# Four units of seven products in each gate and up block, the lows of one pair made by an adding DMA

## The reference, cut to what matters

```
def swiglu(h, w_gate, w_up, w_down):
    return (jax.nn.silu(h @ w_gate) * (h @ w_up)) @ w_down
x = x + mixed
h = rmsnorm(x, ffn_norm[i])
x = x + swiglu(h, ffn_w_gate[i], ffn_w_up[i], ffn_w_down[i])
```

## Time and profile before

| | |
|---|---|
| median of 3 runs | 2096.81 us |
| the profiled execution | 2097.19 us |
| its span, first to last instruction | 2095.3 us |
| granted TensorE clock | 1.0 of full speed |
| busy: PE, DVE, ACT, POOL | 100%, 81%, 66%, 3% |
| DMA, mean busy share of 16 engines | 66.8% (main queue) |

### The profile page before, as it was taken

The page is one execution under the profiler, slowest core; times in us unless marked ns, Lnnn a source line. Parts: engine busy times, 40 slices in busy tenths (PEclk is TensorE's granted clock), DMA queues, the critical chain, the costliest instruction groups (busy, mean ns, idle before and its releaser), DMA issues.

```text
span 2095.3 us, 28360 instructions
## 1 busy us (share of the span) xinstructions
PE 2090.1 (100%) x9733; PEld 1728.8 (83%) x9733; DVE 1687.6 (81%) x2225; ACT 1392.7 (66%) x1890; POOL 65.7 (3%) x39
## 2 busy tenths in 40 slices
PE   9999999999999999999999999999999999999999
PEld 8888888888888888888888888888888888888887
DVE  5776668798988998889767677776889898988888
ACT  6677647576776677656657677665677677777654
POOL 1111000000000000000011101000000000000000
PEclk9999999999999999999999999999999999999999
DMA  8687557676676667665667768675767666666664
GB/s 283 216 231 197 181 168 214 202 221 209 211 226 219 207 208 210 204 214 178 198 211 228 236 219 250 214 231 187 215 217 229 206 214 216 220 214 203 202 200 141
DMA packets 334454, 442.68 MB, mean 211 GB/s; under 512 B 133936, under 2 KB 136720, under 8 KB 334352
## 3 DMA queue, kind: packets, MB, share of 16 engines
q1 hardware_dynamic: 333936, 441.31, 66.8%
q0 software_dynamic: 320, 0.02, 0.0%
q10 hardware_dynamic: 96, 0.03, 0.0%
HBM read 408.27 MB, written 2.10 MB: 196 GB/s over the span
## 4 chain that ended last, share of the span: by engine, by line
PE 99%; DVE 1%; ACT 0%; issue 0%; ACTq 0%
PE work L1942 17%; PE work L1940 17%; PE work L1941 17%; PE acc L1940 15%; PE acc L1942 14%; PE acc L1941 14%; PE work L2105 1%; PE work L2143 1%; PE work L2055 0%; PE work L2116 0%; PE work L2150 0%; PE acc L1929 0%; DVE w_lo L1511 0%; PE work L2119 0%; ACT p_buf L1395 0%; DVE s_buf L1773 0%
## 5 line engine op out<-in xcount | busy, mean ns | idle before, releaser
L1511 DVE TENSOR_TENSOR w_lo<-raw,w_hi 128x1024 fp32r<-128x1024 f32 x756 | 867.4, 1165 | 103.1 <-ACT w_hi L1228 100.0
L1228 ACT ACTIVATE w_hi<-raw 128x1024 fp32r<-128x1024 f32 x756 | 753.8, 1012 | 275.7 <-PE work L1942 155.5
L1940 PE MATMUL work<-w_hi,xT_hi 128*128 128x512 f32 x1516 | 589.9, 389 | 0.0
L1942 PE MATMUL work<-w_hi,xT_lo 128*128 128x512 f32 x1516 | 589.8, 389 | 0.0
L1941 PE MATMUL work<-w_lo,xT_hi 128*128 128x512 f32 x1516 | 589.7, 389 | 0.0
L1940 PE MATMUL acc<-w_hi,xT_hi 128*128 128x512 f32 (+1 forms) x878 | 341.9, 389 | 0.5 <-DVE w_lo L1511 0.5
L1942 PE MATMUL acc<-w_hi,xT_lo 128*128 128x512 f32 (+1 forms) x878 | 338.5, 386 | 0.0
L1941 PE MATMUL acc<-w_lo,xT_hi 128*128 128x512 f32 (+1 forms) x878 | 338.4, 385 | 0.0
L1942 PEld LDWEIGHTS work<-w_hi,xT_lo 128*128 128x128 f32 x1516 | 284.5, 188 | 59.1
L1941 PEld LDWEIGHTS work<-w_lo,xT_hi 128*128 128x128 f32 x1516 | 284.5, 188 | 59.0
L1940 PEld LDWEIGHTS work<-w_hi,xT_hi 128*128 128x128 f32 x1516 | 284.5, 188 | 59.0
(11 more groups left out here) (183 smaller groups left out, 1944.7 us busy)
## 6 DMA issues: line engine op xcount, KB each, us to landing
raw<-in_ffn_w_down_dram SPq DMA_DIRECT2D x176, 512.0 KB, 4.9
raw<-in_ffn_w_gate_dram SPq DMA_DIRECT2D x160, 512.0 KB, 3.8
raw<-in_ffn_w_up_dram SPq DMA_DIRECT2D x160, 512.0 KB, 4.7
raw<-in_odd_w_in_dram SPq DMA_DIRECT2D x48, 1024.0 KB, 5.6
raw<-in_even_w_in_dram SPq DMA_DIRECT2D x32, 1024.0 KB, 5.8
raw<-in_even_w_out_dram SPq DMA_DIRECT2D x16, 1024.0 KB, 5.0
raw<-in_odd_w_out_dram SPq DMA_DIRECT2D x16, 1024.0 KB, 7.0
bias<-in_bias_dram SPq DMA_DIRECT2D x24, 384.0 KB, 3.7
```

The lines of the kernel that those rows point to most:

```text
L1228: act.activation(w_hi[:, s, 0:out], src, ACT.Copy).then_inc(hi_ready, 1)
L1511: dve.tensor_tensor(w_lo[:, s, 0:out], src, w_hi[:, s, 0:out].bitcast(F32), ALU.subtract).then_inc(lo_ready, 1)
L1940: pe.matmul(out_ps, x_hi, wh, start=start, stop=False)
L1942: return pe.matmul(out_ps, x_lo, wh, start=False, stop=stop)
```

## The change: what it does

- `BLOCK` takes the place of `BODY`: pairs 0, 2, 4 and 6 are "eight", pairs 1, 3, 5 and 7 are "seven". A block starts in the ring's order at pair 5 (`FIRST_K`), as before. It has 24 "spots" (halves), numbered 0 to 23 from pair 0 on.
- Pair 0 leaves the rings `w_hi` and `w_lo`. In `negate` ACT copies its raw weights to `added_hi` and again, with scale -1, to `added_lo`, and POOL issues a DMA that adds the raw weights to `added_lo` (128x1024, `accum_op=ALU.add`). DVE does nothing for this pair. The negates stand at spots 18 and 19, six ahead of their use. SP waits for these DMAs, not for `w_lo`, before it loads over pair 0's slot.
- The splits are placed anew (`splits_of_block`), and so are the sums (`sums_of_block`) and the steps of the join (`JOINS`: mix 0 and 1 at spot 0, 2 and 5 at spot 1, 3 at spot 2, 4 and 6 at spot 3, 7 at spot 7). `hidden` stands at spots 6 and 7, `hidden_words` at 12 and 13. SP issues the transpose after the fifth pair of its loop.
- A fourth form takes `hid` as scratch; `added_hi` and part of `added_lo` lie over the attention's buffers, so two loads of `bias` are moved behind layer 0's mixer.

The core of the diff (of the two functions `negate`, the first is POOL's and the second ACT's; `added_half` is PE's):

```diff
-BODY = ("seven", "eight", "seven", "eight", "eight", "eight", "seven", "eight")
+BLOCK = ("eight", "seven", "eight", "seven", "eight", "seven", "eight", "seven")
+ADDED = (0,)
+SPOTS = tuple((k, i) for k, of in enumerate(BLOCK) for i in range(len(PARTS[of])))
+RING = tuple(p for p, (k, _) in enumerate(SPOTS) if k not in ADDED)
+JOINS = ((0, (1,)), (1, (2, 5)), (2, (3,)), (3, (4, 6)), (7, (7,)))
+HIDDEN_MERGES, HIDDEN_WORDS_AT, TURN_WORDS = (6, 7), (12, 13), 4
+def splits_of_block():
+    high, low, whole = {}, {}, len(SPOTS)
+    for i, p in enumerate(RING):
+        k, part = SPOTS[p]
+        at = RING[i - SPLIT] + 1
+        if PARTS[BLOCK[k]][part] in ("sums_a", "sums_b") and k - 1 in ADDED:
+            at += 1
+        high[at % whole] = low[(at + 1) % whole] = PARTS[BLOCK[k]][part]
+    return [high.get(p) for p in range(whole)], [low.get(p) for p in range(whole)]
+NEGATE = {(STARTS[k] - 6 + i + (1 if k else 0)) % len(SPOTS): (k, i) for k in ADDED for i in range(2)}
...
+                def joint(spots, extra, joins=False, more=True):
+                    for p in spots:
+                        k, i = SPOTS[p]
+                        of, last = BLOCK[k], k == SEVENS[-1]
+                        hi, lo = HIGH[p], LOW[p]
...
+                        if joins and p == 0:
+                            mix(0, since=0)
+                        sums_now = SUMS.get(p, ()) if more or p < len(SPOTS) - 2 else ()
+                        for step in sums_now if lo == "one" else ():
+                            make_sums(*step)
+...
+                        if p in NEGATE and (more or NEGATE[p][0]):
+                            negate(*NEGATE[p])
...
+                        for step in sums_now if lo != "one" else ():
+                            make_sums(*step)
+                        extra(p)
...
+            def negate(k, i):
+                pool.wait_ge(negated, e.n.negated.value(1))
+                pool.nop(nofuse=True)
+                pool.dma_start(added_lo[i][:, :].bitcast(F32), raw[:, (FIRST_SLOT + k) % RAW, i * HALF:(i + 1) * HALF],
+                               accum_op=ALU.add).then_inc(low_added[i], 16)
...
+            def negate(k, i):
...
+                act.activation(added_hi[:, i, :], src, ACT.Copy)
+                act.activation(added_lo[i][:, :], src, ACT.Copy, scale=-1.0).then_inc(negated, 1)
...
+            def added_half(i, kt, start, held):
+                pe.wait_ge(low_added[i], n.lows.value(1, unit=16))
+                for w in (1, 0):
+                    wh, wl = (t[:, w * NB:(w + 1) * NB] for t in (added_hi[:, i, :], added_lo[i][:, :]))
```

More of the change, by code:

```diff
@@ L111, in __init__ @@
         self.taken = Count()
+        self.ring = Count()
+        self.negated = Count()
+        self.lows = Count()
+        self.spots = []
         self.x = Count()
@@ L139, in loop @@
                 v.i, v.c, v.per = None, c + rounds * k, 0
+            self.spots = [p + (rounds - 1) * per["half"] for p in self.spots]
 def steps_at(slots, k):
@@ L480, in half @@
                 e.half(hi=hi, lo=lo, **what)
+                if what.get("by_dma") is None:
+                    n.spots.append(n.half.c)
+                    n.ring.c += 1
+                elif what["by_dma"]:
+                    n.lows.c += 1
                 n.half.c += 1
@@ L568, in down_residual, with mix @@
                 n.x.c += 1
-            def mix(i, out=None):
-                e.mix(i, out)
+            def mix(i, out=None, since=None):
+                e.mix(i, out, i + 1 if since is None else since)
                 if i == 5:
@@ L672, in feed_forward, with make_sums, with_up @@
                 n.ffn.c += 1
-                block(1, extra=e.x_forms, added=x0, then="pair")
+                def make_sums(step, since, more):
+                    e.sums(step, since, more)
+                    if step == 2:
+                        n.sums.c += 1
+                def negate(k, i):
+                    e.negate(k, i)
+                    n.negated.c += 1
+                def with_up(k):
+                    e.x_forms(k)
+                    if k == 4:
+                        negate(0, 0)
+                        negate(0, 1)
+                    if k == 5:
+                        e.passed()
+                    if k == 6:
+                        for step in SUMS[len(SPOTS) - 2] + SUMS[len(SPOTS) - 1]:
+                            make_sums(*step)
+                first = PARTS["seven"]
+                block(1, extra=lambda k: with_up(k), added=x0, then=(first[0], first[1], None))
                 e.up(1, acc[2:4])
@@ L682, in stage_low @@
                     n.kt.c += 1
[L684 to L718, removed]
                 def take_words(w):
@@ new lines, in body, with start @@
+                def body(j, merges=HIDDEN_MERGES):
+                    def start(p):
+                        for at, steps in JOINS:
+                            if p == at:
+                                for i in steps:
+                                    mix(i, since=p + 1)
+                        if p in merges:
+                            take_hidden(j, merges.index(p))
+                        words_of(p)
+                    joint(range(FIRST_SPOT, len(SPOTS)), lambda p: None)
+                    joint(range(FIRST_SPOT), start, True)
@@ L834, in second_pass @@
                             n.sets[1].c += 1
-                first_pairs(lambda i: sums_far(i, 5), False)
-                eights((4,), PARTS["seven"][:AHEAD], sums_near)
-                with n.loop(eng, (FB - 3) // 2, half=2 * len(KINDS), made=2 * len(KINDS), raw=32, up=32, sums=6, mix=2, silu=2, direct=2,
+                joint(range(FIRST_SPOT), words_of)
+                with n.loop(eng, (FB - 3) // 2, half=2 * len(SPOTS), made=2 * len(RING), ring=2 * len(RING), raw=32, up=32,
+                            sums=2 * len(SEVENS), mix=2, silu=2, direct=2, negated=4 * len(ADDED), lows=2 * len(ADDED),
                             sets=(0, 4), hT=2) as j:
@@ L992, in chunk, with pair_chunk @@
                 n.half.c += 2
-            def pair_chunk(layer, k, cols, halves, freed, of=(w_gate, w_up)):
-                sp.wait_ge(lo_ready, n.half.value(-freed))
+                n.ring.c += 2
+            def pair_chunk(layer, k, cols, kind, freed, of=(w_gate, w_up), added=None, by_dma=False):
+                if added is not None:
+                    for low in low_added:
+                        sp.wait_ge(low, n.lows.value(-added, unit=16))
+                else:
+                    sp.wait_ge(lo_ready, n.ring.value(-freed))
+                assert not by_dma or n.chunk.slot(RAW) == (FIRST_SLOT + k) % RAW
                 s, u = n.chunk.slot(RAW), n.up.slot(RAW)
@@ L1004, in pair_chunk @@
                 n.up.c += 1
-                n.half.c += halves
+                n.half.c += len(PARTS[kind])
+                n.ring.c += 0 if by_dma else len(PARTS[kind])
+                n.lows.c += int(by_dma)
             def columns(w, cols, which=range(KT // 4), after=None):
@@ L1225, in split @@
                 if n.made.past(SPLIT):
-                    act.wait_ge(half_used, n.made.value(1 - SPLIT))
+                    act.wait_ge(half_used, n.half.value(n.spots[n.made.c - SPLIT - n.ring.c] - n.half.c + 1))
                 out, src = split_views(kind, s, r)
@@ L1560, in x_forms, with mix @@
                     last.then_inc(flo_ready, 1)
-            def mix(i, out):
+            def mix(i, out, since):
                 n = e.n
@@ L2020, in half @@
                      added=None, hi=None, lo=None, kt=None, direct_stop=False,
-                     part=None, f=None, layer=None, held=False, first_sets=False, first=False, last=False, closes=False,
-                     staged=None, begins=False, columns=None):
+                     part=None, f=None, layer=None, held=False, first=False, last=False, closes=False,
+                     staged=None, begins=False, columns=None, by_dma=None):
                 n = e.n
-                s = n.half.slot(SPLIT)
+                if by_dma is not None:
+                    return added_half(by_dma, kt, start, held)
+                s = n.ring.slot(SPLIT)
                 if part is not None:
```

231 lines of the change are left out of this document (139 added, 92 removed).

## The result

The changed kernel takes 2142.58 us (2140.90 to 2148.18) against 2096.81 before: ratio 1.0223 [1.0203, 1.0242]. Slower was right; 2119 was not, and the range ended at 2137. Of the 45.8 us the prediction had found 22.

A forecast was written before the change was run, and what follows sets the result against it. PE bounds the kernel before; after, a DVE-ACT circle of 42.9 us a block. Per layer 1.25 + 16.7 us lost less 6.8 saved is 11.2, 22.3 in two, on 2097.19, median 0.4 lower: 2119 us, range 2092 to 2137.

The forecast's parts named there:

- PE's own period, 13.6 us saved: Gate and up blocks: 180 matmuls instead of 183, 40.80 us a block, 0.68 us less in each of 20 blocks.
- The circle of DVE and ACT: Steady blocks: 38.5 us of DVE work plus 4.3 of waits for ACT make the period 42.9 us; chance 0.67.
- the negate between highs 22 and 23: ACT's order at the block's end: `negate(0, 1)`, 1.92 us, ahead of high 23, was called the deciding step.
- The burst: DVE's gapless work from spot 23 to spot 10, 20.1 us, would delay PE by 1.05 to 1.25 us a block.
- I take 6 us ... so nothing shows: Landing time chosen for pair 0's adding DMAs, with ends of 3.8 and 9.1 us; PE would not wait.
- 8.1 us: Room for the second add before spot 1: 6.4 us from its issue, plus 1.7 for PE coming late.
- the rival: Adds land late and PE waits for them at spots 0 and 1, deciding from 8.1 us on; chance 0.09.
- 10 us by the same rule: The late-adds case at spots 0 and 1: a landing of 10 us was said to give 2155 us.
- under 5: Argument against late adds: transfers of 512 KB in the blocks were said to take under 5 us.
- Costs one for one: PE's wait for late adds at spots 0 and 1 would lengthen the time by its full length, from 8.1 us on.
- The half rate of an adding transfer: Adding DMAs: each piece needs two reads, so 512 KB takes about twice as long, still inside 8 us.
- The load of pair 4 and the transpose cost nothing: SP's queue: pair 4's load, after both adds, has 5 us to land; the load behind the transpose is due at 36.

The follow-up runs named there:

- e6: Changed kernel with both negates after high 21, `hidden_words` one spot earlier, a layer's first negates before `x_forms`, pair 3's load waiting for both adds: 2097.65 us.
- e11: Changed kernel with one edit: on SP, pair 3's load waits for both adds of its block instead of running beside them; 2117.21 us.
- e1: Changed kernel with the adding DMA cut from 1024 to 16 columns, leaving pair 0's lows incomplete; 2116.98 us.
- e2: Changed kernel with both negates after high 21, so that none stands between highs 22 and 23; 2114.50 us.
- e8: Changed kernel with three sevens instead of four (pair 1 an eight, words at spots 10 and 11), adding DMAs kept; 2171.14 us.
- e3: Changed kernel with `hidden_words` one spot earlier, at spots 11 and 12, ahead of the sums' high 16; 2143.52 us.
- e5: Changed kernel with negates after high 21, `hidden_words` one spot earlier, a layer's first negates before `x_forms`, adding DMA cut to 16 columns: 2097.47 us.

## Why the prediction was right and where it was wrong

- **PE's own period, 13.6 us saved**: right by the count, 180 matmuls of 0.2267, and hidden in every steady block, where the circle sets the pace; in e6 the period is back at 41.58, with 0.7 of PE's waits over it.
- **The circle of DVE and ACT**: right. Period 42.9 walked, 42.72 measured in e11, with idle times of 0.35, 1.27 and 2.2 us against 0.45, 1.5 and 2.4. The sum, 2119, fits e1 and e11, 2117, within 2 us. That the negate between highs 22 and 23 decides was right too: e2's period is 0.9 us under e11's.
- **The burst**: right in its places. In e11 PE starts late at spots 23 (0.66), 6, 8 and 10 (0.57, 0.17 and 0.18, together 0.92, where the walk had 1.05). It had nothing at spot 3, where PE starts 0.21 late behind a step of the join.
- **"I take 6 us ... so nothing shows"**: this step failed, in both its numbers. The landing of the second add was 7.8 us, inside the ends of 3.8 and 9.1, but I had set the value by size alone and had not laid SP's loads beside it, though I had written that two adds and the loads of pairs 1 to 3 fall in the same time. And the room was not 8.1 us: issued at 541.29 and wanted at 547.41 it had 6.1. I had added 1.7 for PE's being late to a window that was counted from DVE's times and had that delay in it. With 6.1 the chosen value of 6 would have been on the edge, and the rival would have had far more than 0.09. Two slips beside it changed nothing: 10 us by the same rule gives 2153, not 2155, and "under 5" is true of the medians, while 7 of 75 up loads before took up to 5.8.
- **"Costs one for one"**: wrong, and only partly in the kernel's favour. Of a wait of 1.74 a steady block shows 0.56 more period (43.28 against 42.72), since PE's waits at spots 6 and 10 go, and what re-enters the circle is the late high 6, DVE's 0.45. But in some blocks the clock falls behind the gap, and the period is 45 to 46. From `low_a`'s first issue to its last, layer 0 takes 7.6 us more than in e11 and layer 1 10.8; the remaining 5 of the 23.6 us between the two spans lie outside, the wait for the first add of layer 0 and the ends of the layers among them.
- **The half rate of an adding transfer**, which the Trainium skill states in "Collectives: The Full Stack", under the bandwidth ceiling: the prediction let it change nothing, but it belongs in the sum of what fills the engines. The trace agrees with it in the engines' time, 5.0 us against 2.7 for a MB in e11, and the DMA share of a block rises from 0.67 of 41.48 us to 0.78 of 42.72, 5.5 us more, as for an add that costs twice a load. The landing hides it: beside no load an add of 512 KB lands in 4.4 us, where loads take 3.9 and 5.0. What it costs shows when the engines have no time to spare.
- **The load of pair 4 and the transpose cost nothing**: right, and of pair 3's load too: in e11 it leaves 10.5 us behind pair 2's instead of 2.9, and the whole run has one wait of 0.3 us for a load.

## What to carry to other kernels

A transfer that is moved onto the path has two numbers, landing and room, and both come from laying all queues side by side at that time, with the time that each transfer holds the engines, not from its size; where its landing decides, a load that has slack is to wait for it. An order of two engines that hand each other work is walked start by start, and its period can exceed the busier engine's work by the idle time that the order makes (4.3 of 42.9 us here); that engine's sum of work alone doesn't forecast it (35.5 us of work and a period of 44.5 in e8). A wait taken from one place of such a circle often comes up in the next, so causes are taken away together (e2 and e3 against e6) before a gain is written off.

## What the runs showed of the hardware

A gap on PE costs more than its length when the granted clock falls behind it. PE of the changed kernel at the start of layer 1:

```profile
1465.83 0.50 PE L2048 MATMUL work<-added_hi,xT_hi 128*128 128x512 f32 x1 [3.12 <-DMA low_a<-raw]
...
1467.21 0.63 PE L2050 MATMUL work<-added_hi,xT_lo 128*128 128x512 f32 x1
1467.64 0.63 PE L2048 MATMUL work<-added_hi,xT_hi 128*128 128x512 f32 x1
```

After 3.12 us without work five starts lie 0.23 to 0.35 apart, the next seven 0.43, at 1.2 GHz instead of 2.4: about 1.6 us beyond the gap. In e3 a wait of 2.09 us was followed by the same. The length alone didn't decide: in the changed kernel the clock stayed at 1.0 behind the 1.74 us shown above and behind 2.15 (at 420.03), and fell to 0.5 behind 1.96 (at 722.18). Small adds were not free either: 8 KB on POOL's queue landed after 3.0 to 5.1 us (e1, e5), much of what 512 KB took in e11.
